# The first layer's last six up tiles as seven block products, the modulation tiles and three small loads moved

## The reference, cut to what matters

```python
mods = silu(c) @ w_mod[layer] + b_mod[layer]
shift1, scale1, gate1, shift2, scale2, gate2 = split(mods, 6)
h = rmsnorm(x, g_attn[layer]) * (1 + scale1) + shift1
x = x + gate1 * mixer_layer(h, ...)
h = rmsnorm(x, g_mlp[layer]) * (1 + scale2) + shift2
u, g = split(h @ w_up[layer], 2)            # 1024 -> 2 x 2816
g = causal_depthwise_conv(g, conv_w[layer], conv_b[layer])   # three taps
x = x + gate2 * ((silu(g) * u) @ w_down[layer])
```

## Time and profile before

| what | value |
|---|---|
| median of three runs | 1941.82 us (1941.79 to 1944.37) |
| the profiled execution, its own time | 1944.36 us |
| its span in the profile | 1942.6 us |
| PE, DVE, ACT, POOL busy | 85%, 36%, 15%, 7% of the span |
| first layer: first up matmul to first down matmul | 184.9 to 346.5 us |
| second layer: first up matmul to first down matmul | 555.8 to 702.0 us |

### The profile page before, as it was taken

How to read it: one execution, slowest core, us unless ns; L and a number is a source line. 1 busy time by engine, 2 the same in 40 slices (tenths; PEclk the granted TensorE clock), 3 DMA queues, 4 the chain that set the end, 5 groups by cost and what they waited for, 6 DMA issues and landing times.

```text
span 1942.6 us, 24583 instructions
## 1 busy us (share of the span) xinstructions
PE 1657.2 (85%) x10484; PEld 945.1 (49%) x10484; DVE 708.4 (36%) x1470; ACT 283.5 (15%) x761; POOL 143.7 (7%) x151
## 2 busy tenths in 40 slices
PE   8999999999999999999785766758999785756757
PEld 3455988544579964474432232322574432232322
DVE  1584566977528976273010010101174110010101
ACT  1243000021511001252000010001253000010000
POOL 0011000000213510310000000000220000000000
PEclk9999999999999999999897887979999997987978
DMA  9991888755235643646999999999845999999998
GB/s 353 328 350 59 261 292 298 277 202 187 88 110 187 233 152 125 201 174 241 402 428 430 428 432 425 433 429 409 266 174 216 404 429 430 426 432 427 432 429 352
DMA packets 165957, 599.76 MB, mean 309 GB/s; under 512 B 20977, under 2 KB 79857, under 8 KB 142065
## 3 DMA queue, kind: packets, MB, share of 16 engines
q1 hardware_dynamic: 165630, 598.04, 78.4%
q10 hardware_dynamic: 242, 0.53, 0.1%
HBM read 594.76 MB, written 3.80 MB: 308 GB/s over the span
## 4 chain that ended last, share of the span: by engine, by line
PE 57%; DMA 38%; DVE 3%; ACT 2%; issue 1%; POOL 0%; SPq 0%; DVEq 0%; ACTq 0%
DMA extra<-in_w_down 14%; DMA extra<-in_w_up 12%; DMA extra<-in_w_gate 11%; PE ps L1266 9%; PE ps L1379 6%; PE ps L1332 6%; PE ps L1304 5%; PE ps L1625 5%; PE ps L949 4%; PE ps L1118 4%; PE ps L1517 3%; PE ps L1216 3%; PE ps L1645 1%; DMA ring<-in_w_mod 1%; PE ps L835 1%; PE ps L857 1%
## 5 line engine op out<-in xcount | busy, mean ns | idle before, releaser
L1625 PE MATMUL ps<-ring,wide 128*32 128x256 f32 x2912 | 219.7, 468 | 117.4 <-DMA ring<-in_w_up 72.4
L1625 PEld LDWEIGHTS ps<-ring,wide 128*32 128x32 f32 x2912 | 107.7, 133 | 223.2 <-DMA ring<-in_w_up 81.8
L1645 PE MATMUL ps<-ring,wide 128*32 128x512 f32 x768 | 157.4, 638 | 45.7 <-DMA ring<-in_w_down 45.7
L3212 DVE TENSOR_TENSOR wide<-ps,wide 128x512 f32<-128x512 f32 x16 | 10.7, 670 | 508.8 <-PE ps L1625 508.8
L1266 PE MATMUL ps<-hT,ring 128*128 128x256 f32 (+1 forms) x1088 | 183.8, 330 | 0.0
L1266 PEld LDWEIGHTS ps<-hT,ring 128*128 128x128 f32 x1088 | 166.6, 191 | 17.3 <-issue 2.9
L1625 PE MATMUL ps<-extra,wide 128*32 128x256 f32 x1056 | 91.4, 519 | 63.6 <-DMA extra<-in_w_up 38.7
L1379 PE MATMUL ps<-ring,hT 128*128 128x512 f32 (+2 forms) x320 | 127.3, 555 | 0.4 <-issue 0.4
L1645 PEld LDWEIGHTS ps<-ring,wide 128*32 128x32 f32 x768 | 44.7, 116 | 154.4 <-issue 126.4
L2384 DVE SCALAR_TENSOR_TENSOR extra<-ring,sc,extra 128x512 f32<-128x512 f32 x140 | 109.8, 785 | 5.2
L1625 PEld LDWEIGHTS ps<-extra,wide 128*32 128x32 f32 x1056 | 42.9, 147 | 111.0 <-DMA extra<-in_w_up 42.5
(11 more groups left out here) (373 smaller groups left out, 2098.6 us busy)
## 6 DMA issues: line engine op xcount, KB each, us to landing
ring<-in_w_gate SPq DMA_DIRECT2D x24, 4096.0 KB, 31.4
ring<-in_w_down SPq DMA_DIRECT2D x24, 4096.0 KB, 33.6
ring<-in_w_up SPq DMA_DIRECT2D x20, 4096.0 KB, 32.9
ring<-in_w_mod SPq DMA_DIRECT2D x24, 2048.0 KB, 13.4
ring<-in_w_up SPq DMA_DIRECT2D x44, 1024.0 KB, 8.0
extra<-in_w_gate SPq DMA_DIRECT2D x8, 4096.0 KB, 35.1
extra<-in_w_up SPq DMA_DIRECT2D x8, 4096.0 KB, 33.1
ring<-in_w_in SPq DMA_DIRECT2D x13, 2048.0 KB, 12.6
```

The source lines that it names most:

```text
L1625: last = mm(ps[2 * part + e // 2][j * CAP:(j + 1) * CAP, e % 2 * 2 * P:(e % 2 + 1) * 2 * P], xsT[:, k, e * CAP:(e + 1) * CAP], expert_row( ...
L1645: last = mm(ps[6 + n][e * CAP:(e + 1) * CAP, :], hidT[:, e, k, :], expert_row(n0, e, k)[:, n * N:(n + 1) * N], start=k == 0, stop=k == KD - 1)
```

## The change

1. `UP_WHOLE` becomes (5, 2): up tiles 5 to 10 of the first layer run in seven block products, as tiles 2 to 10 of the second do already.
2. Twelve modulations of the first layer move in the tile list, and so in the DMA, DVE and PE programs. They follow hand-written tables: `FOLD_AFTER` (place in the tile list and of PE's fold), `SUM_WHOLE`, `SUM_FIRST` and `SUM_PARTS` (DVE's accumulation, whole or by ranges of its eight steps), and `READ_AFTER` (`mod_out`). accumulate(10) to (13) go among DVE's work at the end of "out". Three buffers take turns (`mod_sum`), and banks 4 and 6 take the folds up to q = 18 (`mod_bank`).
3. The gate bias is loaded ahead of up tile 2 in place of 8; the bias copies and the router ahead of up tile 8 in place of 4.
4. In both layers the tap with the bias moves from DVE to ACT (`tap`), and in seven-product tiles the convolution of tile j - 1 stands at the start of tile j. `up_second` and `up_rows_sums` stand ahead of the convolution of the last whole tile.
5. On POOL the weight sums of the first layer stand ahead of the scaling of the router.

```diff
-UP_WHOLE = (11, 2)
-LAGS = (2, 6)
+UP_WHOLE = (5, 2)
+FOLD_AFTER = ({("out", 1): (10, 11), ("up", 1): (12, 13), ("up", 2): (14, 15), ("up", 3): (16,), ("up", 4): (17, 18),
+               ("up", 7): (19,), ("up", 9): (20,), ("down", 2): (21,)}, {("up", 6): (0,), ("up", 7): (1,)})
+READ_AFTER = ({1: (12, 13), 2: (14, 15), 3: (16,), 8: (19,), 10: (20,)}, {6: (0,), 7: (1,)})
+SUM_WHOLE = {0: (14,), 1: (15,), 2: (16, 17), 3: (18,)}
+SUM_FIRST = ({5: (19, range(0, 2)), 6: (19, range(4, 6)), 7: (20, range(0, 2)), 8: (20, range(4, 6))}, {})
+SUM_PARTS = ({5: (19, range(2, 4)), 6: (19, range(6, 8)), 7: (20, range(2, 4)), 8: (20, range(6, 8))},
+             {3: (0, range(0, 3)), 4: (0, range(3, 6)), 5: (0, range(6, 8)), 6: (1, range(0, 4)), 7: (1, range(4, 8))})
...
-                if (L, kind, j) == (0, "up", 4):
+                if (L, kind, j) == (0, "up", 8):
                     sp.wait_ge(sems["rpb_loaded"], 16)
                     sp.dma_start(copies.rearrange("l h c m -> (l h) c m"),
...
-                if (L, kind, j) == (0, "up", 8):
+                if (L, kind, j) == (0, "up", 2):
                     sp.wait_ge(sems["b1_mix_added"], 4)
...
                     for m in UP_STEPS:
-                        if j > 2:
-                            pe.wait_ge(*up_read(s, m, j - 1))
+                        if j > first:
+                            pe.wait_ge(*up_read(s, L, m, j - 1))
+                        elif m == 6 and L == 0:
+                            pe.wait_ge(*s.at("b1_mod_ready", FOLD_AFTER[0][("up", first - 1)][-1] + 1))
                         elif m == 5:
-                            pe.wait_ge(*s.at("b1_product_ready", 2))
+                            pe.wait_ge(*s.at("b1_product_ready", first - first % 2))
+                        elif m == 3:
+                            pe.wait_ge(*s.at("b1_product_ready", first - 1 + first % 2))
...
+                def tap(j):
+
+                    y = sm[:, j % 2, :].rearrange("p (f t) -> p f t", f=2)
+                    act.wait_ge(*up_block(s, L, 4, j))
+                    gp = ps[2 * (j % 2) + 1][:, :].rearrange("p (f t) -> p f t", f=2)
+                    if j >= UP_WHOLE[L]:
+                        act.wait_ge(*up_read(s, L, 4, j))
+                        gp = up_joined(j)[:, 1, :, :]
+                    for f in range(2):
+                        av(y[:, f, :], gp[:, f, :], ACT.Identity, scale=cc1(L, "conv_w", 2 * FCH + 2 * j + f),
+                           bias=cc1(L, "conv_b", 2 * j + f)).then_inc(s.up("b1_up_by_act" if f else None), 1)
...
                 out_residual(0, 0)
+                if L == 0:
+                    accumulate(10)
                 out_residual(0, 1)
                 norm_stream(which, 0)
                 out_residual(1, 0)
                 evac_stream(which, 0, 24)
+                if L == 0:
+                    accumulate(11)
                 out_residual(1, 1)
                 norm_stream(which, 1)
                 evac_stream(which, 1, 24)
+                if L == 0:
+                    accumulate(12)
+                    mod_out(10)
+                    accumulate(13)
+                    mod_out(11)
...
+                first = UP_WHOLE[L]
+                for j in range(first - 1):
+                    conv(j)
+                    up_gated(j)
+                    if L == 0:
+                        for q in SUM_WHOLE[j]:
+                            accumulate(q)
+                up_second(first)
+                up_rows_sums()
                 if L == 0:
-                    mod_out(EARLY[L] + UPT - LAGS[L])
+                    mod_out(17)
+                    mod_out(18)
+                for j in range(first, UPT):
+                    if j in SUM_FIRST[L]:
+                        accumulate(*SUM_FIRST[L][j])
+                    conv(j - 1)
+                    up_join(j, UP_READS[:1])
+                    up_fourth(j)
+                    up_gated(j - 1)
+                    if j in SUM_PARTS[L]:
+                        accumulate(*SUM_PARTS[L][j])
+                    if j == UPT - 1:
+                        down_sums(0)
+                    up_join(j, UP_READS[1:])
+                conv(UPT - 1)
+                up_gated(UPT - 1)
+                down_sums(1)
                 down_sums(2)
                 down_sums(3)
                 if L == 0:
-                    accumulate(EARLY[L] + UPT)
-                    mod_out(EARLY[L] + UPT + 1 - LAGS[L])
+                    accumulate(21)
                 down_sums(5)
                 down_sums(4)
```

More of the change, by code:

```diff
@@ L90, in _b1_tiles @@
                 tiles += [(0, "mod", q) for q in MOD_AT[i]]
[L91 to L94, removed]
+        tiles.append((l, "out", 0))
+        for t in [(l, "out", 1)] + [(l, "up", j) for j in range(UPT)] + [(l, "down", j) for j in range(NDOWN)]:
             tiles.append(t)
-            if LAGS[l] <= n < len(late) + LAGS[l]:
-                tiles.append((late[n - LAGS[l]][0], "mod", late[n - LAGS[l]][1]))
+            tiles += [(MODS[l][q][0], "mod", MODS[l][q][1]) for q in FOLD_AFTER[l].get(t[1:], ())]
     return tiles
@@ L124, with _up_acts @@
 TAB = {}
+def _up_acts(l):
+    first = UP_WHOLE[l]
+    acts = [(what, j) for j in range(first - 1) for what in ("tap", "silu")]
+    for j in range(first, UPT):
+        acts += [("tap", j - 1), ("copy", j), ("silu", j - 1)]
+    return acts + [("tap", UPT - 1), ("silu", UPT - 1)]
+UP_ACTS = [_up_acts(l) for l in range(DEPTH)]
+UP_SEVEN = [UPT - UP_WHOLE[l] for l in range(DEPTH)]
 def _tab():
@@ L1349, in _ @@
                     last.then_inc(tile_done, 1)
-                    if UPT + j - LAGS[L] < late:
-                        modulation(EARLY[L] + UPT + j - LAGS[L])
+                    folds(("down", j))
                 for j in DOWN_TAIL:
@@ L1927, in _, with up_copies @@
                     av(pT[:, j % 2, :], sm[:, j % 2, :], ACT.Silu).then_inc(s.up("b1_up_by_act"), 1)
+                def up_copies(j):
+                    act.wait_ge(*up_block(s, L, 1, j))
+                    if j >= UP_WHOLE[L] + 2:
+                        act.wait_ge(*s.at("b1_product_ready", j - 1))
+                    for c in range(2):
+                        av(up_joined(j)[:, :, 0, c * P:(c + 1) * P], ps[UP_BANK[1]][:, 0:T].rearrange("p (h t) -> p h t", h=2),
+                           ACT.Copy).then_inc(s.up("b1_up_by_act" if c else None), 1)
+                for what, j in UP_ACTS[L]:
+                    if what == "tap":
+                        tap(j)
+                    elif what == "silu":
+                        silu(j)
+                    else:
+                        up_copies(j)
                 if L == DEPTH - 1:
@@ L2873, in _ @@
-                if L == 0:
-                    mod_out(EARLY[L] + UPT - LAGS[L])
+                    for q in READ_AFTER[L].get(j, ()):
+                        mod_out(q)
+                first = UP_WHOLE[L]
+                for j in range(first - 1):
[6 more added lines that the diff above has]
+                up_rows_sums()
```

197 lines of the change are left out of this document (86 added, 111 removed).

## The result

The changed kernel took 1954.78 us (median of four runs, 1951.33 to 1957.45) beside 1943.09 for the kernel before (1941.79 to 1944.74): ratio 1.0059, 95% interval 1.0047 to 1.0071. It is slower by 0.6%, and outside the predicted range.

A forecast was written before the change was run, and what follows sets the result against it. PE was taken to bound the touched stretch, as long as DVE and the ring's loads keep up. Up of layer 0 +3.9 (stalls +10.5 included), down -1.1, layer 1 -1.6: +1.2 on 1941.8, 1943.0 us; range 1936.5 to 1947.5.

The forecast's parts named there:

- The two places (tiles 5 and 7): Layer 0's up: PE stalls 4.7 in tile 5 for modulation 19 and 5.8 in tile 7 for modulation 20.
- down's -1.1: Down of layer 0, whose end DVE sets: 1.1 shorter, with accumulate(20) gone from it.
- -7.8 + 1.6 + 10.5: Layer 0's up: six seven-product tiles save 7.8, two more folds cost 1.6, the two stalls 10.5.
- (c): Rival: DVE beside POOL becomes the bound of layer 0's tiles 5 to 8; +4.6, 1946.4; chance 0.22.
- When mod 20 lands: Layer 0's tile 7: modulation 20, behind bias copies and router, lands at 302.8 (301 to 305); DVE's chain ends at 307.7.
- Stall 5.8: Layer 0's tile 7: PE needs product 3's input at 301.9, has it at 307.7; 5.8 lost (0 to 8).
- the 0.06 for a longer stall: Chance of 0.06 left for a stall in layer 0's up longer than its bounds.
- cost nothing: Layer 0: accumulations between up tiles need 3.2 + 6.0 of DVE (12 for two) within PE's 13.8 per tile; no loss.
- -1.6 forecast: Layer 1's seven products: DVE's chain to product(1) ends 2.1 sooner, 0.5 given back at the fold after tile 7.
- 0 to 0.3 per tile, hidden unless DVE is late: Seven-product tiles: DVE may wait 0.9 for ACT's tap where it worked 0.8, costing 0 to 0.3 per tile.
- (a): Rival: modulation 20 lands by 297.0, so tile 7's stall is gone; -4.6, 1937.2; chance 0.16.
- (b): Rival: neither modulation load holds DVE in layer 0's up; -9.3, 1932.5; chance 0.12.

The follow-up runs named there:

- pe_filled_2: Changed kernel with six unread matmuls on PE ahead of every wait of product 3 in layer 0's tiles 5 and 7; 1952.16 us, ratio 1.0046.
- pool_later: Changed kernel with POOL's sums for layer 0's up tile 8 held until DVE finished the fourth sum of tile 7; 1950.19 us, ratio 1.0045.
- tap_on_dve: Changed kernel with the tap of seven-product tiles back on DVE, in both layers; 1952.08 us, ratio 1.0051.
- both_late_tap: both_late with the tap of seven-product tiles back on DVE, in both layers; 1941.51 us, ratio 1.0000.
- router_late: Changed kernel with the router alone loaded later, ahead of down tile 1, the bias copies staying ahead of up tile 8; 1951.66 us, ratio 1.0050.
- loads_late: Changed kernel with the bias copies and router moved from ahead of up tile 8 to ahead of down tile 1; 1949.51 us, ratio 1.0039.
- sum20_late: Changed kernel with only the parts of modulation 20's sum one tile later (tiles 8 and 9); 1947.74 us, ratio 1.0026.
- pe_filled: Changed kernel with six unread matmuls on PE at layer 0's tiles 5 and 7, in tile 5 behind the wait; 1957.08 us, ratio 1.0076.
- sums_late: Changed kernel with DVE's sums of modulations 19 and 20 one tile later, all loads unmoved; 1938.53 us, ratio 0.9980.
- both_late: Changed kernel with the sums of modulations 19 and 20 one tile later and bias copies and router ahead of down tile 1; 1938.16 us, ratio 0.9976.

## Why the prediction was wrong

**What held.** The two places (tiles 5 and 7), the two loads named for them, the order of the chain behind each landing, PE's idle time (5.7 for 4.7, 5.9 for 5.8), the router and copies as what delays modulation 20, the tile of 12.5, down's -1.1 (-1.15), the wait in layer 1's tile 2 gone. DVE waited 5.14 and 5.30 for the two tiles; for the second, 6 to 9 had been given as the sign. The first down matmul was forecast at 350.4 and came at 356.25 + 1.92 = 358.2. Of the total miss (+1.2 forecast, +10.9 to +11.7 in the medians) this is 7.8. (The prediction's terms, -7.8 + 1.6 + 10.5, make +4.3 and not the +3.9 of the schedule laid by hand; the 0.4 changes nothing below.) The miss has three terms, read at tile 7, whose end does not hang on what PE lost before it, as pe_filled_2 shows:

- **The landing of modulation 20**: DVE starts on it at 302.06 + 1.92 = 304.0, forecast 302.8. +1.2, inside the bounds given (301 to 305).
- **The chain behind it**, forecast as 4.9 from rows in which DVE worked alone: 8.6 measured (302.06 to 310.67), +3.7. All of it is the convolution, 5.69 beside POOL's sums for tile 8. pool_later took it away with the landing where it was. The prediction did weigh DVE beside POOL, but only in rival (c), for the four steps of an accumulation; the short chain on which the stall's end hangs was priced without it. The Trainium skill (SBUF - State Buffer, "SBUF: two separate sides") states that a DVE instruction with two SBUF inputs and a GpSimd one hold their shared port for a whole instruction, each blocking the other. The trace agrees here: the four instructions lost 3.9 beside POOL's of about 1.4 each (2.72 for two), and nothing once POOL came later. In tile 5 the same operation had one input in PSUM (ps) and lost nothing beside POOL:

```profile
273.32 1.77 DVE L2835 SCALAR_TENSOR_TENSOR spare<-ps,fixed,spare 128x255 f32<-128x255 f32 x4
```

```profile
272.81 2.94 POOL L2279 TENSOR_TENSOR ring<-ring 128x512 f32<-128x512 f32 x2
```

- **The products behind the wait**, which the prediction did not price at all: a stall was counted as its idle time. +2.55 in tile 7, at a granted clock of 0.50. (Tile 5's +2.1 only makes PE later for a landing that it would have waited for.)

1.2 + 3.7 + 2.55 = 7.5 of the 7.8. So the **step that failed** is the paragraph "When mod 20 lands", with its "Stall 5.8": the chain behind the landing was priced at 4.9 and took 8.6, and the slow products behind the wait, 2.55, were put at nothing. Its idle time was right only by luck, because two errors cancelled. PE came to it at 304.77 + 1.92 = 306.7, not 301.9 (DVE had modulation 19 at 273.2 and not at 271.3, the chain behind it took 6.2 for 5.6, with one step of 1.63 beside POOL, and the slow products cost 2.1), and the stall's end moved from 307.7 to 312.6 as well. Both idle times lay inside their bounds, so even the 0.06 for a longer stall did not cover what happened.

**accumulate(18)**, one of those that "cost nothing", made PE wait 0.80 at fold 18. In the changed kernel this only shortened PE's wait in tile 5; in the versions without stalls it is a loss (0.77 to 1.06). Seven steps beside POOL's first sums took 9.03 where the earlier trace rows has 5.48:

```profile
252.62 9.03 DVE L2451 SCALAR_TENSOR_TENSOR extra<-ring,sc,extra 128x512 f32<-128x512 f32 x7
```

**Layer 1: -1.6 forecast, -0.54 measured.** The 2.1 and more at its start came. What I gave back for a late DVE, 0.5, was 1.68: "0 to 0.3 per tile, hidden unless DVE is late" is 0.34 per tile (1.64 less 1.30), which over five tiles is 1.7, and tap_on_dve, where the 1.68 is gone, shows that it is this handover.

**The rivals.** (a) and (b) did not happen. (b) had 9.3 below before for a kernel without stalls; once the sums stand a tile later, 4 below was measured (1938), so (b) promised too much. (c) was right in its sign, and by its own mechanism, a late DVE, it appears in both_late_tap and, in small, in the waits of 0.7 to 1.05 in tiles 8 and 9 of router_late and pool_later; in the changed kernel the stalls hide it. The 7.8 in layer 0 and the 1.1 in layer 1 make 8.9 of a miss of 9.7 to 10.5 in the medians. The remaining 1 or so isn't settled: the profiled execution is the fastest of its kernel, and the falls of the clock described below may be in the others.

## What to carry to other kernels

On an engine that works in order, put the first use of a tile that arrives from memory behind the work that the matmul engine waits for, or a round later: here moving the same sums by one tile was worth 14.7 us, and without it the whole change was a loss. Price a stall of TensorE with what follows it (here 2.1 and 2.6 of slow products behind 5.7 and 5.9 of idleness), and price the chain behind a landing with the neighbour that works at that moment, not alone. Handing a small operation to another engine pays where other work fills the handover (layer 0) and costs where nothing does (layer 1).

## What the runs showed of the hardware that was not expected

- **The granted clock behind waits.** 0.50, that is 1.2 GHz, behind waits of 5.69, 5.90, 6.25, 6.73, 6.93 and 3.99; 1.00 (2.4 GHz) behind 1.72 and behind 2.10 that followed six filler matmuls. Behind the same wait of 1.98 to 1.99 at the end of down the first matmuls took 1.98 in some kernels and 2.55 to 3.33 in five others (loads_late, sum20_late, router_late, pe_filled, tap_on_dve).
- **Falls far from the edit.** The stretch "between" is the same program in all kernels and took 161.65 to 161.94 in five profiled executions and 163.30 to 166.64 in the nine others; in loads_late, where it took 166.63, the clock was 0.50 for 4 us in it. All nine have such a stretch at the same place of layer 1's attention, 108 to 110 behind the last wait of down, and the five just named also the slow matmuls at the end of down. In this way 3.0 to 4.7 of the gains of 3.0, 4.5 and 7.4 in "up 0" were given back in pe_filled_2, router_late and loads_late. Each figure is of one execution; whether a kernel has the fall in all of its executions, and what decides it, stays open. The Trainium skill (TensorE: Matmul & The Clock Gate, "What's actually happening") has the clock set by how busy the engine has been, with the moment of a change varying from run to run of one kernel. The long waits agree with the first. For the second only the changed kernel was profiled twice: the clock fell at the same two waits, and what followed differed a little (product 3 of tile 5 took 3.79 and 3.62, product 4 of tile 7 2.73 and 2.34).
- **DVE beside POOL.** The same four instructions: 1.78 to 1.79 alone, 5.69 beside POOL, where each of POOL's pairs took 2.7 to 2.8; 1.77 beside POOL where one input came from PSUM. One wait that kept the two apart took 3.9 off.
- **The copy from SBUF to DRAM of 2.7 MB.** In sums_late and both_late PE is at the same point, and they differ in the place of the copy and the router alone: modulation 20 was issued at 285.71 and 274.73 and was in 15.9 and 13.2 later: 119.8 and 106.0 after the first up matmul (181.82 and 181.91). The router alone, moved away, made 1.8 at the landing and nothing at the issue, though the longest issue of the queue, 14.12, had stood in its name.
